# Decay rows of the second attention, spread over the partitions: by DMA through DRAM in place of products with a column of the identity

## The reference

```
b     = cumsum(log_f)                                 # running sum of the forget gate
log_w = where(s <= t, b[t] - b[s] + i[s], -inf)
m_t   = max over s of log_w (and of the carried state)
a     = (q @ k.T) * exp(log_w - m_t)
h     = (a @ v) / max(|sum(a)|, exp(-m_t))
```

## Time and profile before

| | |
|---|---|
| median of three runs | 873.16 us |
| the profiled execution | 877.62 us |
| its span, first to last instruction | 875.8 us |
| TensorE busy | 88% of the span |
| VectorE / ScalarE / GpSimd busy | 61% / 45% / 28% |
| stage of both attentions | 223 to 377 us |
| mean granted TensorE clock | 0.930 of full speed |

### The profile page before, as it was taken

One profiled execution on the slowest core, in us unless ns is written; L12 is line 12 of the kernel. 1 busy time (PEld: TensorE's weight loads), 2 busy tenths in 40 slices (PEclk: granted clock), 3 DMA queues, 4 the chain that ended last, 5 costly groups with the idle time before them and its releaser, 6 DMA issues.

```text
span 875.8 us, 10161 instructions
## 1 busy us (share of the span) xinstructions
PE 770.1 (88%) x3824; PEld 611.0 (70%) x3824; DVE 533.6 (61%) x640; ACT 395.4 (45%) x464; POOL 241.4 (28%) x126
## 2 busy tenths in 40 slices
PE   4598999969999999989899967899999999999830
PEld 2375777747788888848777836788887788888620
DVE  1354643360344454469540786888888888888827
ACT  1342222312424243352221535767777667777514
POOL 0252242323123222324564621212223322220030
PEclk9599999989799999999999957999999999999965
DMA  9877556447121121162270058799999999995343
GB/s 323 271 212 245 166 169 210 156 144 218 47 73 49 49 73 49 49 250 76 64 270 28 25 192 310 304 366 385 375 384 391 379 374 363 387 384 223 141 160 155
DMA packets 74975, 185.81 MB, mean 212 GB/s; under 512 B 13970, under 2 KB 44794, under 8 KB 68796
## 3 DMA queue, kind: packets, MB, share of 16 engines
q1 hardware_dynamic: 66912, 162.60, 52.5%
q0 software_dynamic: 4272, 11.31, 3.8%
q10 hardware_dynamic: 3756, 11.41, 3.2%
HBM read 172.72 MB, written 16.78 MB: 216 GB/s over the span
## 4 chain that ended last, share of the span: by engine, by line
PE 54%; DVE 20%; issue 14%; ACT 5%; DMA 4%; POOL 2%; ACTq 1%; SPq 1%; POOLq 0%; DVEq 0%
PE psum L714 40%; DVE moe_low L2055 11%; ACT half_high L1400 2%; DMA xbuf<-x_sample 2%; PE psum L785 2%; PE psum L947 2%; PE psum L885 2%; PE psum L810 1%; PE psum L767 1%; PE psum L927 1%; DVE slot L1636 1%; PE psum L906 1%; PE psum L897 1%; DVE xsT_low L2064 1%; PE psum L795 1%
## 5 line engine op out<-in xcount | busy, mean ns | idle before, releaser
L2172 POOL TENSOR_TENSOR low_ring<-front_ring,high_ring 128x1024 fp32r<-128x1024 f32 x54 | 130.8, 2424 | 318.9 <-ACT high_ring L1209 318.9
L1209 ACT ACTIVATE high_ring<-front_ring 128x1024 fp32r<-128x1024 f32 x54 | 57.1, 1058 | 234.8 <-PE psum L714 201.6
L714 PE MATMUL psum<-h_low,high_ring 128*128 128x512 f32 x312 | 118.0, 395 | 0.0
L714 PE MATMUL psum<-h_high,high_ring 128*128 128x512 f32 x312 | 117.0, 392 | 0.0
L714 PE MATMUL psum<-h_high,low_ring 128*128 128x512 f32 x280 | 114.3, 408 | 1.1 <-POOL h_low L2180 0.5
L2055 DVE TENSOR_TENSOR moe_low<-front_ring,half_high 128x2048 fp32r<-128x2048 f32 x48 | 107.9, 2285 | 10.4 <-ACT half_high L1400 10.4
L714 PE MATMUL psum<-half_high,xsT_low 128*128 128x512 f32 x256 | 103.4, 404 | 10.4 <-DVE xsT_low L2064 6.2
L714 PE MATMUL psum<-half_high,xsT_high 128*128 128x512 f32 x256 | 101.9, 398 | 0.0
L714 PE MATMUL psum<-moe_low,xsT_high 128*128 128x512 f32 x256 | 101.9, 398 | 0.0
L1400 ACT ACTIVATE half_high<-front_ring 128x2048 fp32r<-128x2048 f32 x48 | 91.0, 1914 | 8.5 <-PE psum L714 8.5
L2055 DVE TENSOR_TENSOR moe_low<-slots,half_high 128x2048 fp32r<-128x2048 f32 x32 | 73.1, 2286 | 13.0 <-ACT half_high L1400 13.0
(11 more groups left out here) (284 smaller groups left out, 1325.6 us busy)
## 6 DMA issues: line engine op xcount, KB each, us to landing
front_ring<-w_down SPq DMA_DIRECT2D x16, 2048.0 KB, 11.6
front_ring<-w_in SPq DMA_DIRECT2D x34, 512.0 KB, 5.6
xbuf<-ada_w SPq DMA_DIRECT2D x32, 512.0 KB, 4.2
slot<-w_gate SPq DMA_DIRECT2D x8, 2048.0 KB, 10.1
front_ring<-w_up SPq DMA_DIRECT2D x8, 2048.0 KB, 9.8
slots<-w_up SPq DMA_DIRECT2D x8, 2048.0 KB, 9.9
slots<-w_gate SPq DMA_DIRECT2D x8, 2048.0 KB, 10.6
y_rows<-inout ACTq DMA_DIRECT2D x16, 512.0 KB, 11.3
```

Source lines behind the costliest of these rows:

```text
L714: mm = pe.matmul(out, lhs(a, k), rhs(b, k), start=(start and k == 0 and a == 1), stop=(stop and k == count - 1 and (a, b) == (0, 0)))
L1209: act.activation(dst, src.rearrange("p (k n) -> p k n", k=KD), ACT.Copy).then_inc(high_ready, 1)
L2172: pool.tensor_tensor(low, src, high.bitcast(F32), ALU.subtract).then_inc(low_ready, 1)
```

## The change

The row products and their eight PSUM groups go. In their place SyncE, behind the load of piece bg0.1, stores the two decay rows of each head to a buffer in DRAM (`run_rows`, 4 x 2 x 512 floats, 16 KB), waits until gateT is made and the store has landed, and issues eight loads, one for each unit. Each reads the unit's two rows of 256 floats 128 times over, once for each partition, and writes them to `run_wide`, which covers the whole of `slot3` (256 KB each, 2 MB in all). VectorE's `decays` waits for the landing of its unit's load and reads the row from SBUF. ScalarE's exponential waits for a semaphore of its own in place of the emptied bank.

```diff
--- before.py
+++ after.py
@@ -183,10 +183,10 @@
     for b in range(TT):
         bg = [(f"bg{4 * b + n}", "s") for n in range(4)]
         g += [(f"score{b}.{j}", "v") for j in range(PAIRS)]
-        g += [(f"mrow{2 * b}", "v"), (f"qk{2 * b}", "v"), bg[0], bg[1]]
+        g += [(f"qk{2 * b}", "v"), bg[0], bg[1]]
         g += [(f"pT{b}.{n}", "vs"[n % 2]) for n in range(4)]
         g += [(f"num{2 * b}.0", "v"), (f"num{2 * b}.1", "v")]
-        g += [(f"mrow{2 * b + 1}", "v"), (f"qk{2 * b + 1}", "v"), bg[2], (f"pv{b}", "v")]
+        g += [(f"qk{2 * b + 1}", "v"), bg[2], (f"pv{b}", "v")]
         g += [(f"num{2 * b + 1}.0", "v"), (f"num{2 * b + 1}.1", "v"), bg[3], (f"oT{b}", "s")]
     g += [(f"spread{b}.{r}", "s") for b in range(4, 10) for r in range(REQS)]
     g += [(f"upa{j}", "v") for j in range(KD)]
@@ -294,6 +294,7 @@
         eps = sb("eps", [P, 1])
 
         psum = ctx.enter_context(nc.psum_tensor("psum", [P, BANKS, COLS], F32))
+        run_rows = nc.dram_tensor("run_rows", [M_HEADS, 2, TOK], F32, kind="Internal").ap()
         h2_rows = nc.dram_tensor("h2_rows", [TOK, D], F32, kind="Internal").ap()
         y_rows = nc.dram_tensor("y_rows", [2 * MAX_PAIRS * P, D], F32, kind="Internal").ap()
 
@@ -312,6 +313,8 @@
         rows = slot3[0:M_HEADS, 0:2048].rearrange("p (g t) -> p g t", g=4)
         rows_x = slot3[0:M_HEADS, 2048:3072].rearrange("p (g t) -> p g t", g=2)
         ones_row = slot3[0:M_HEADS, 3072:3328]
+
+        run_wide = slot3[:, :].rearrange("p (u d t) -> p u d t", u=2 * M_HEADS, d=2)
         bgate = slots45[:, :, :].rearrange("p s (c t) -> p (s c) t", t=TOK)
         probs = xbuf[:, :, :].rearrange("p (b a) n -> p b (a n)", b=2).rearrange(
             "p b (h k) -> p b h k", h=A_HEADS)
@@ -435,6 +438,9 @@
         negmax_ready = sem("negmax_ready")
         probs_ready = sem("probs_ready")
         decay_ready = sem("decay_ready")
+        run_stored = sem("run_stored")
+        run_landed = [sem(f"run_landed{u}") for u in range(2 * M_HEADS)]
+        decay_sum = sem("decay_sum")
         hm_sq = sem("hm_sq")
         hm_root = sem("hm_root")
         hm_ready = sem("hm_ready")
@@ -656,6 +662,16 @@
                                  .rearrange("(s p) d -> p s d", p=P),
                                  og[:, 0:2, :].rearrange("p a b -> p (a b)").rearrange("p (s d) -> p s d", s=1)
                                  .to_broadcast([P, 2 * (MAX_PAIRS - MIN_PAIRS), D])).then_inc(zeros_stored, 16)
+                if piece == ("bg0", 1):
+
+                    sp.wait_ge(rows_ready, 1)
+                    sp.dma_start(run_rows, rows[:, 2:4, :]).then_inc(run_stored, 16)
+                    wait_full(sp, "gateT")
+                    sp.wait_ge(run_stored, 16)
+                    for u in range(2 * M_HEADS):
+                        r, h = u // M_HEADS, u % M_HEADS
+                        sp.dma_start(run_wide[:, u], run_rows[h:h + 1, :, r * SEQ:(r + 1) * SEQ]
+                                     .to_broadcast([P, 2, SEQ])).then_inc(run_landed[u], 16)
 
 
             def expert(s):
@@ -891,13 +907,6 @@
             def mlstm_scores(u):
 
                 r, h = u // M_HEADS, u % M_HEADS
-                name = f"mrow{u}"
-                wait_bank(pe, name)
-                for d in range(2):
-                    mm = pe.matmul(bank(name)[:, d * SEQ:(d + 1) * SEQ],
-                                   ident[0:M_HEADS, h:h + 1].to_broadcast([M_HEADS, P]),
-                                   rows[:, 2 + d, r * SEQ:(r + 1) * SEQ], start=True, stop=True)
-                mm.then_inc(psum_full, 1)
                 if u == 0:
                     pe.wait_ge(conv_done, 8)
                 name = f"qk{u}"
@@ -1294,7 +1303,7 @@
                 act.activation(st[:, 4, :], st[:, 2, :], ACT.Exp).then_inc(probs_ready, 1)
 
             def decay_exp(u):
-                wait_emptied(act, f"mrow{u}")
+                act.wait_ge(decay_sum, u + 1)
                 act.activation(ebuf[:, u % 2], ebuf[:, u % 2], ACT.Exp).then_inc(decay_ready, 1)
 
             for b in range(TT):
@@ -1715,12 +1724,11 @@
                     wait_full(dve, f"num{u - 2}.1")
                 if u == 0:
                     wait_emptied(dve, "gateT")
-                name = f"mrow{u}"
-                wait_full(dve, name)
+                dve.wait_ge(run_landed[u], 16)
                 e = ebuf[:, u % 2]
                 L, U = const("maskL"), const("maskU")
                 for d in range(2):
-                    m = bank(name)[:, d * SEQ:(d + 1) * SEQ]
+                    m = run_wide[:, u, d, :]
                     for s in range(TPR):
                         wide = s == d
                         col = gateT[:, 0, d, r * TPR + s, h:h + 1]
@@ -1731,7 +1739,7 @@
                         ins = dve.scalar_tensor_tensor(
                             out=e[:, d, 0:SEQ] if wide else e[:, d, SEQ:SEQ + P],
                             in0=m if wide else m[:, own], scalar=col, in1=mask, op0=ALU.add, op1=ALU.add)
-                emptied(ins)
+                ins.then_inc(decay_sum, 1)
 
             def weigh(u):
 
```

## The result

| | before | changed |
|---|---|---|
| median of 20 runs | 878.02 us (867.54 to 881.84) | 870.80 us (867.18 to 873.30) |
| the profiled execution | 877.62 us, span 875.8 | 871.12 us, span 867.7 |

A forecast was written before the change was run, and what follows sets the result against it. TensorE was taken to bound the second attention stage, so its removed row products gave 9.35 us and all else 0: 873.16 less that is 863.8 us, 1.07% faster. Its own range was 857 to 870, the wider one 855 to 874.

The forecast's parts named there:

- TensorE bounds the stage: Second attention, 223 to 377 us: TensorE ends every wait, so removing its row products saves their 9.35 us.
- The sum's term: Row products removed from TensorE in the second attention: 2.00 + 7 x 1.05 = 9.35 us, the only term.
- my two cases: First row products in the slow clock spell: 2.00 us won, 9.35 in all, or only 1.05, 8.40 in all.
- The other engines keep up: Softmax and VectorE's weighing in the second attention stay ahead of TensorE, with margins of 3.4 us and more; cost 0.
- bank rotation: Eight fewer PSUM groups pass through the eight banks in the second attention; nothing waits longer, cost 0.
- SBUF reads: VectorE's 32 decay additions read SBUF in place of PSUM; 0 on each, upper end 2.35 us if GpSimd blocks.
- The loads are hidden: Store lands by 216 us, eight spreading loads by about 225, bg0.2 by 229; nobody waits, cost 0.
- Rival A: Spreading loads at 57 GB/s delay bg0.2; TensorE idles 13.8 us, kernel 4.5 us slower at 877.6; 7%.
- all of it moves with the stage: Behind the second attention, TensorE's 3.2 us idle and the expert-weight loads shift along with it; nothing given back or added, 0.
- Rival C: More than the sum: slow spell ends earlier or a later one is missed, bringing it to 860.5 us; 6%.
- The base: Whole kernel: forecast taken from a median of three, 873.16 us, with runs spread from 868.19 to 879.13.

The follow-up runs named there:

- e3: Changed kernel with the row products put back on constants, VectorE still reading its rows from SBUF: 878.96 us, ratio to the kernel before 1.0026.
- e14: Changed kernel with filler products at both gaps, one at 221 us and three behind the second attention: 863.93 us, ratio to the kernel before 0.9868.
- e2: Changed kernel, unedited, run and profiled again beside the kernel before: 868.0 us, ratio 0.9892; its profiled execution 863.4 us.
- e15: Changed kernel with only the one filler product at the 221 us gap: 866.02 us, ratio to the kernel before 0.9885.
- e4: Changed kernel with three filler products in the 3.2 us gap behind the second attention: 863.84 us, ratio to the kernel before 0.9856.
- e7: Changed kernel with VectorE making all diagonals of the spreading products ahead of the attention output's low parts: 869.65 us.
- e9: Kernel before with one filler product at the 221 us gap: 873.28 us, ratio to the kernel before 0.9957.
- e13: Kernel before with both fillers, one product at 221 us and three behind the second attention: 873.68 us, ratio to the kernel before 0.9989.
- e8: Changed kernel with VectorE making all diagonals of the spreading products first, plus one filler product at 221 us: 867.10 us.

## Why the prediction was right or wrong, point by point

- *TensorE bounds the stage; the products are worth what they take.* Right (e3, e14). The sum's term was 9.35 us. At equal clock it is 9.2; in the two profiles the stage lost 10.8. That 9.35 and 9.2 lie so close is in part luck. The odd units brought 1.25 us each where the rows said 1.05: the hidden weight load, which I had not counted. The first row products, 2.00 us in a spell, are 1.05 without one. In the first profile the spell brought the rest: scores 0.18, the first row products 2.00, and 0.48 on the 48 products. The sum there is the upper of my two cases and a little more, but neither case is what the clock did. It rose at about 231.2, 1.4 us after the 48 products began and not 2.5, and 3 us earlier than before; the spell lasted 6.8 us, not 10.2. In e2 there is none.
- *The other engines keep up; bank rotation costs nothing; SBUF reads cost nothing.* Right. TensorE has no idle time in the stage. The first decay needed no landing, and the decays met no pass of GpSimd. The Trainium skill, "Vector Engine (DVE) Microarchitecture Reference", section "Points that are easy to get wrong", says that this form runs at half throughput with two SBUF sources that are not bf16. The trace does not agree: 1.40 us for four, in place of 1.39 with one of the sources in PSUM.
- *The loads are hidden.* Right: store landed by 215.6 (forecast 216), the eight landed 3.3 to 6.3 us after issue, bg0.2 waited for by nobody. Rival A's price was too high. The spreading loads ran far faster than its 57 GB/s: issued from 215.56 to 219.3, the last had landed by 225.6 at the latest, 2 MB in 10 us.
- *Behind the stage "all of it moves with the stage ... Nothing is given back, nothing added."* This is the step that failed. No wait gave it back, but the clock did. I had looked at the spell at 223 only, and taken the clock behind the stage as fixed. In the three profiles with the row products gone and the gap behind the attention left as it was (the first, e2, e15), a spell stands at 370 to 378, on products that are on the chain; in none of the eight profiles of the kernel before does one, nor in e3. It cost 2.4 us in the first profile, 1.1 in e2 and 1.2 in e15. With the gap filled it is gone (e4, e14), and the time from the stage's end to the weights' products is the 15.5 us of the kernel before. In the first profile the account is full: the stage ends 10.6 us earlier, 2.4 are given back behind it and 1.6 outside the span, and 6.5 are left. For the medians it is only likely: the spell was seen in profiles, not in the twenty timed executions, and of what lies outside the span their medians have 0.3. Rival C foresaw a spell of such a size with the wrong sign.
- *The base.* 863.8 was worked out from a median of three, 873.16. Twenty give 878.02. The three held one execution of the group near 868 and two of the other (873.16 and 879.13), which the range of 868.19 to 879.13 showed and the text treated as spread of one kind. The lower group, 15 of 84 executions, also pulls the ratio toward 1; the changed kernel's twenty have no such second group. What makes it stays open: eight profiles of the kernel before didn't catch one, and with both fillers 2 of 12 executions still took 866.5.

Open too: why the spell at 223 stood in all eight profiles of the kernel before, and in only one of four of the changed kernel and its variants without the filler at 221 (it stood in the first, not in e2, e4 and e7). e3, with the products put back and the eight loads kept, has it, which speaks against the loads as what takes it away. The fillers show that it goes when the gap at 221 is filled (e9 and e13, against eight of eight without), not why it comes more in the one kernel than in the other. The gap of 3.2 us behind the attention is in both kernels. Why a spell follows it in the changed kernel and in e9, and never in the kernel before as it was, is open as well.

## What to carry to other kernels

Here work taken from the engine that ends every wait of a stage was worth its own time at full clock, 8.4 us, and 0.8 more for the weight loads that it had kept from overlapping. 2 MB of loads cost nothing that shows, put ahead of a piece that was taken up 16 us after its own issue. How much of the saving is seen depends on what TensorE's clock does at the idle gaps around it: price the products behind each gap at both clock levels, and put both prices in the range. A gap that another engine causes can be filled with products that nobody reads; the changed kernel with such fillers has the lowest medians here, 863.84 us (e4) and 863.93 (e14), against 878 for the kernel before and 868 to 871 for the changed one. Take the base from enough executions to see whether they make one group or two.

## What the runs showed of the hardware

- Behind an idle gap of 0.9 us on TensorE, at 221 us, a spell at 1.2 GHz of 10.2 us stood in eight of eight profiles of the kernel before; with a product in the gap it was gone (e9, e13), and the stage 4.9 us shorter for a filler of 1.05 us. In the changed kernel one of four had it without the filler, and none with it (e8, e14, e15).
- Behind an idle gap of 3.2 us, at the end of the attention, a spell stood in three of three profiles of the changed kernel that left the gap and none with products in it (e4, e14); in the kernel before the same gap had none, eight times, and one with the filler at 221 us (e9). The gap alone doesn't make the spell.
- Two executions of the same code lay 7.7 us apart (871.1 and 863.4). Of this 4.6 us come from two spells, in the stage and behind it, and 1.4 lie outside the span.
- A 128x8 addition of two SBUF operands on VectorE took 1.60 us, until a pass of GpSimd ended; 128x512 operations that met such a pass took 2.8 us in place of 0.7.
- Spreading rows of DRAM over 128 partitions, in runs of 1 KB, took 3.3 to 6.3 us for 256 KB with eight such loads in flight.
